# Expert weights in three 2 MB transfers per expert in place of ten

## What is computed

```python
xb = h[slot_tok].reshape(n_blocks, DISPATCH_BLOCK, D)
def expert_block(args):
    xe, e = args
    hid = jax.nn.silu(xe @ w_gate[e]) * (xe @ w_up[e])
    return hid @ w_down[e]
```

## Time and profile before

| | us |
|---|---|
| median of three runs (1152.67 to 1154.23) | 1153.86 |
| the profiled execution's own time | 1153.56 |
| its span | 1151.8 |
| TensorE matmuls busy in it | 1075.8 (93%) |
| 16 DMA engines, SyncE's queue | 62.6% of the span |

### The profile page before, as it was taken

The page is one execution under the profiler, slowest core; times in us unless marked ns, Lnnn a source line. Parts: engine busy times, 40 slices in busy tenths (PEclk is TensorE's granted clock), DMA queues, the critical chain, the costliest instruction groups (busy, mean ns, idle before and its releaser), DMA issues. The chain is left out here.

```text
span 1151.8 us, 17851 instructions
## 1 busy us (share of the span) xinstructions
PE 1075.8 (93%) x5269; PEld 616.3 (54%) x5270; DVE 513.6 (45%) x665; ACT 510.6 (44%) x690; POOL 290.6 (25%) x308
## 2 busy tenths in 40 slices
PE   5999996998999878999999999999999999969996
PEld 4899985877887532333333333333333333328885
DVE  5488999885232352123113213212311313356886
ACT  5444546663321264335345435535533625424332
POOL 2168776784000101011101011101111101023320
PEclk9999997999999788999999999999999999989999
DMA  8211941302132939999999999999999999965541
GB/s 264 66 55 39 287 129 74 116 19 92 74 135 90 345 141 394 396 376 338 398 395 357 396 397 362 398 398 386 369 396 396 364 395 399 403 222 188 194 147 41
DMA packets 149297, 300.32 MB, mean 261 GB/s; under 512 B 12032, under 2 KB 42784, under 8 KB 149259
## 3 DMA queue, kind: packets, MB, share of 16 engines
q1 hardware_dynamic: 134907, 264.69, 62.6%
q0 software_dynamic: 6512, 22.29, 5.6%
q10 hardware_dynamic: 7840, 12.85, 3.0%
HBM read 261.72 MB, written 38.06 MB: 260 GB/s over the span
## 5 line engine op out<-in xcount | busy, mean ns | idle before, releaser
L2012 PE MATMUL ps_gate_up<-weights,x_turned 128*64 128x512 f32 x1568 | 349.6, 598 | 1.7 <-issue 1.0
L106 ACT COPY weights<-raw_weights 128x2048 f32 (+1 forms) x99 | 186.0, 1899 | 102.7 <-issue 46.9
L2012 PEld LDWEIGHTS ps_gate_up<-weights,x_turned 128*64 128x64 f32 x1568 | 109.6, 137 | 207.2 <-issue 206.1
L106 DVE COPY weights<-raw_weights 128x2048 f32 x93 | 114.4, 1231 | 216.9 <-PE ps_gate_up L2012 83.0
L2025 PE MATMUL ps_y<-weights,h_turned 128*64 128x512 f32 x784 | 179.0, 598 | 0.9 <-ACT h_turned L1932 0.9
L439 POOL TENSOR_TENSOR conv_pool_taps<-conv_pool_taps,tap_product 128x448 f32<-128x448 f32 (+1 forms) x88 | 135.9, 1544 | 39.1 <-ACT tap_product L540 28.9
L115 POOL COPY token_ids<-item_tokens 128x1 int32 (+1 forms) x48 | 8.8, 183 | 446.2 <-PE ps_x L1999 446.2
L1972 DVE TENSOR_TENSOR hidden<-ps_gate_up,act_gate 128x256 f32<-128x256 f32 x49 | 20.8, 425 | 223.5 <-ACT act_gate L1923 210.6
L879 DVE SCALAR_TENSOR_TENSOR taps_bank<-a_ext,par,taps_bank 128x640 f32<-128x640 f32 (+1 forms) x128 | 101.5, 793 | 3.3
L2025 PEld LDWEIGHTS ps_y<-weights,h_turned 128*64 128x64 f32 x784 | 52.2, 136 | 93.3 <-issue 92.2
L540 ACT ACTIVATE tap_product<-a_ext,par 128x448 f32<-128x448 f32 (+1 forms) x104 | 75.4, 740 | 50.8 <-POOL conv_pool_taps L439 34.1
(11 more groups left out here) (285 smaller groups left out, 1560.2 us busy)
## 6 DMA issues: line engine op xcount, KB each, us to landing
raw_weights<-w_exp_gate SPq DMA_DIRECT2D x128, 512.0 KB, 12.0
raw_weights<-w_exp_up SPq DMA_DIRECT2D x128, 512.0 KB, 12.8
raw_weights<-w_exp_down SPq DMA_DIRECT2D x64, 1024.0 KB
y_rows<-y_tile ACTq DMA_DIRECT2D x98, 128.0 KB, 5.4
y_rows<-zero_rows SPq DMA_DIRECT2D x16, 512.0 KB, 6.2
x_rows<-x_tile SPq DMA_DIRECT2D x9, 512.0 KB, 2.6
h_rows<-h_tile SPq DMA_DIRECT2D x9, 512.0 KB, 2.9
mixer<-x_rows SPq DMA_DIRECT2D x9, 512.0 KB, 4.5
```

Of the source, the lines that this page charges most:

```text
L106: copy(S.work[s][:, :], raw).then_inc(S.w_ready[s], 1)
L2012: last = pe.matmul(ps_gu[side[j], :, :], x_t[:, c, side[of]], w[:, :, share(D_EXP, j)], start=(k == 0), stop=(k == KD - 1))
```

## The change

Gate and up of an expert come in two transfers of 2 MB (gate first, then up) which share one semaphore, and down comes in one of 2 MB with its own. All four copies of gate and up wait for both transfers of their group, both copies of down for theirs. SyncE issues the group of gate and up only when all four pieces of expert n-2 were copied and the whole group of n-1 has landed, and down in the same way. In `routing`, all of gate and up of expert 1 is issued at the late place, and down alone at the early one. The bytes, the rows of 2 KB (gate, up) and 4 KB (down) in `raw_weights`, and the copies stay.

```diff
+FIRST_OF = (0, 0, 0, 0, 4, 4)
...
-def load_piece(eng, S, s, n, slot, e):
-
+def load_weights(eng, S, pieces, n, slot, e):
+
+    first = pieces[0]
     if type(n) is not int or n >= 1:
-        eng.wait_ge(S.raw_loaded[s], n * LANDED[s])
+        eng.wait_ge(S.raw_loaded[first], n * LANDED[first])
+    for s in pieces:
+        if type(n) is not int:
+            eng.sem_inc(S.waits_met, 1)
+        if type(n) is not int or n >= 2:
+            eng.wait_ge(S.w_ready[s], n - 1)
...
+    raw = S.raw[:, slot, pieces[0]:pieces[-1] + 1, :].rearrange("p s n -> p (s n)")
+    if pieces == GU:
         for m in range(2):
-            eng.dma_start(raw.rearrange("p (k m n) -> p k m n", k=2, m=2)[:, :, m, :],
-                          S.w_experts[m][0, e, rows, :].rearrange("o (k p) n -> p (o k) n", p=P)).then_inc(S.raw_loaded[s], 16)
+            eng.dma_start(raw.rearrange("p (k m n) -> p k m n", k=KD, m=2)[:, :, m, :],
+                          S.w_experts[m][0, e, :, :].rearrange("o (k p) n -> p (o k) n", p=P)).then_inc(S.raw_loaded[first], 16)
     else:
...
+        eng.dma_start(raw.rearrange("p (k n) -> p k n", k=KE),
+                      S.w_experts[2][0, e, :, :].rearrange("o (k p) n -> p (o k) n", p=P)).then_inc(S.raw_loaded[first], 16)
...
-    eng.wait_ge(S.raw_loaded[s], n * LANDED[s] + LANDED[s])
+    eng.wait_ge(S.raw_loaded[FIRST_OF[s]], n * LANDED[s] + LANDED[s])
...
-                for s in (3, 4, 5):
-                    load_piece(sp, S, s, 1, 1, slice(1, 2))
+                load_weights(sp, S, DOWN, 1, 1, slice(1, 2))
...
-                for s in (0, 1, 2):
-                    load_piece(sp, S, s, 1, 1, slice(1, 2))
+                load_weights(sp, S, GU, 1, 1, slice(1, 2))
...
-                        for s in PIECES:
-                            load_piece(sp, S, s, n + odd, odd, bass.ds(e, 1))
+                        for pieces in (GU, DOWN):
+                            load_weights(sp, S, pieces, n + odd, odd, bass.ds(e, 1))
```

More of the change, by code:

```diff
@@ L72 @@
 PIECES = GU + DOWN
+FIRST_OF = (0, 0, 0, 0, 4, 4)
 LANDED = (32, 32, 32, 32, 16, 16)
-def load_piece(eng, S, s, n, slot, e):
+def load_weights(eng, S, pieces, n, slot, e):
+    first = pieces[0]
     if type(n) is not int or n >= 1:
-        eng.wait_ge(S.raw_loaded[s], n * LANDED[s])
+        eng.wait_ge(S.raw_loaded[first], n * LANDED[first])
[4 more added lines that the diff above has]
+            eng.wait_ge(S.w_ready[s], n - 1)
     if type(n) is not int:
         eng.sem_inc(S.waits_met, 1)
[L82 to L88, removed]
+    raw = S.raw[:, slot, pieces[0]:pieces[-1] + 1, :].rearrange("p s n -> p (s n)")
+    if pieces == GU:
         for m in range(2):
-            eng.dma_start(raw.rearrange("p (k m n) -> p k m n", k=2, m=2)[:, :, m, :],
-                          S.w_experts[m][0, e, rows, :].rearrange("o (k p) n -> p (o k) n", p=P)).then_inc(S.raw_loaded[s], 16)
-    else:
[L93 to L96, removed]
+            eng.dma_start(raw.rearrange("p (k m n) -> p k m n", k=KD, m=2)[:, :, m, :],
+                          S.w_experts[m][0, e, :, :].rearrange("o (k p) n -> p (o k) n", p=P)).then_inc(S.raw_loaded[first], 16)
+    else:
+        eng.dma_start(raw.rearrange("p (k n) -> p k n", k=KE),
+                      S.w_experts[2][0, e, :, :].rearrange("o (k p) n -> p (o k) n", p=P)).then_inc(S.raw_loaded[first], 16)
 def copy_piece(eng, S, n, s, items, on_act=None):
-    eng.wait_ge(S.raw_loaded[s], n * LANDED[s] + LANDED[s])
+    eng.wait_ge(S.raw_loaded[FIRST_OF[s]], n * LANDED[s] + LANDED[s])
     if items is not None:
@@ L379, in _ @@
                         sp.wait_ge(o_left, BLOCKS * PARTED)
-                        for s in PIECES:
-                            load_piece(sp, S, s, 0, 0, slice(0, 1))
+                        for pieces in (GU, DOWN):
+                            load_weights(sp, S, pieces, 0, 0, slice(0, 1))
                 for j in range(3):
@@ L1859, in _ @@
                         e = sp.value_load(S.expert_at[0:1, bass.ds(n + odd, 1)], min_val=0, max_val=EXPERTS - 1)
-                        for s in PIECES:
-                            load_piece(sp, S, s, n + odd, odd, bass.ds(e, 1))
+                        for pieces in (GU, DOWN):
+                            load_weights(sp, S, pieces, n + odd, odd, bass.ds(e, 1))
                 for s in range(4):
                     sp.wait_ge(w_ready[s], EXPERTS - 1)
-                    sp.wait_ge(S.raw_loaded[s], LANDED[s] * EXPERTS)
+                    sp.wait_ge(S.raw_loaded[0], LANDED[0] * EXPERTS)
                     sp.dma_start(S.raw[:, 0, s, :].rearrange("p (k n) -> p k n", n=D), ple_gate[:, 2 * s:2 * s + 2, :])\
@@ L1936, in gate_hi @@
                 def gate_hi(s):
-                    act.wait_ge(S.raw_loaded[s], LANDED[s] * EXPERTS + 16)
+                    act.wait_ge(S.raw_loaded[s], 16)
                     act.wait_ge(w_ready[s], EXPERTS)
@@ L1984, in _ @@
                 for n, s in enumerate((0, 1)):
-                    dve.wait_ge(S.raw_loaded[s], LANDED[s] * EXPERTS + 16)
+                    dve.wait_ge(S.raw_loaded[s], LANDED[0] * EXPERTS + 16 if s == 0 else 16)
                     dve.wait_ge(w_ready[s], EXPERTS)
```

## The result

The kernel with three transfers took 1199.63 us (median of 4 runs, 1197.57 to 1201.97) against 1153.26 us for the kernel before (4 runs, 1150.84 to 1154.23): 46.4 us more. The ratio on record is 1.0413 with a 95% interval of 1.0397 to 1.0429 (the two medians alone give 1.040). The forecast was 1188 us, with a range of 1168 to 1204. The profiled execution has a span of 1197.2 us, 45.4 above the 1151.8 of before. Lines 2012, 2032, 1972, 1923 and 1905 of before are 2010, 2030, 1970, 1921 and 1903 now.

What follows compares the result with a forecast made beforehand. The prediction took TensorE's own work as the bound, transfers only just quick enough. Terms 28.4 + 2.3 + 5 - 0.7 = 35 us on 1153.9 gave 1189, lowered by 1 for waits already there to 1188 us; range 1168 to 1204.

Steps and rivals of the forecast that it cites:

- Six tight places: Items 9, 17, 25, 33, 41 and 47: TensorE would idle 4 to 6 us ahead of the transposes there.
- The six places, 28.4 us: Next item starts 4.3 us late at four of the waits for weights, 5.6 at two: 28.4 us together.
- The fourth piece: At each of six waits, no copy starts before all four gate and up pieces land: 2.6 us each.
- the later issue of down: At each of six waits, down's issue also waits for VectorE's copy: 1.1 us, or 0 if the queue isn't dry.
- the second copy: At each of six waits, ScalarE's copy 0 now also comes behind the last landing: 1.9 us each.
- slack: Delay a landing can take before TensorE waits: 1.3 us at four of the six waits, 0 at two.
- The start, 2.3: Expert 1's gate and up land later with a fourth piece, delaying items 1 and 2: 2.3 us, 5 if later still.
- The clock, 0.8 a place, 5 us: TensorE's clock may fall behind each of six idle waits: 0.8 us each, 5 us in all, bounds 0 and 13.8.
- a full loss of the clock, 1197 us: Case where full clock loss alone, bounded by 2.3 us at each of six waits, gives 1197 us.
- The end, -0.7: At the barrier behind the stage, SyncE's last transfers and ScalarE's last store pass the delay through; 0.7 us taken off.
- SyncE's issues, 0: On SyncE, 3 issues per expert in place of 10 free a queue that nobody waits for: 0 us.
- The rival of a dry queue: Transfer queue runs dry between groups, 3 to 7 us a round more: 1205 to 1225 us, chance 0.13.

Runs made afterwards that it cites:

- silu ahead, ten transfers: Kernel before, ten transfers and a signal per piece, with silu, next tokens' copy and product put ahead of the copies for the next expert: 1151.59 us.
- the copies held back: Kernel before, its ten transfers issued as before, but each copy waits until all pieces of its group (gate and up, or down) have landed: 1183.75 us.
- every wait and ten transfers: Kernel before, ten transfers; copies wait for their whole group's landing, issues for its copying, and expert 1's piece 3 is issued late: 1193.85 us.
- the run with copy 2 moved: The changed kernel with ScalarE's copy 2 placed behind silu, the next tokens and copy 4; copy 0 stays ahead of silu: 1189.64 us.
- the run that held back only the issue: Kernel before, ten transfers; no piece of a group is issued before all pieces of that group in the same slot were copied: 1153.53 us.
- down alone joined: Kernel before with only down in one 2 MB transfer with one signal; gate and up stay in eight transfers with four signals: 1153.94 us.

## Why the prediction was right, and where it was not

- *TensorE bounds, the transfers are only just quick enough.* Right. With the waits gone (silu ahead, ten transfers) the stage runs at 11.56 us an item and not faster.
- *Six tight places, and only items 0 and 1 else.* Right: the waits stand at items 9, 17, 25, 33, 41 and 47 and at item 0.
- *The six places, 28.4 us.* 32.4 came. The terms can be read one by one from the start of ScalarE's first copy behind the landing. Counted from the start of its item and summed over the six places, it is 43.2 us before (the third piece), 57.5 with the copies held back, 63.0 with every wait and ten transfers, and 67.5 in the change:

| term at the six places | forecast, us | measured, us |
| --- | --- | --- |
| the fourth piece | 15.6 | 14.2 |
| the later issue of down | 6.6 | 5.6 |
| the size of the transfers | none | 4.5 |
| the second copy | 11.4 | 10.9 |
| slack | -5.2 | -2.9 |
| sum | 28.4 | 32.3 (32.4 but for rounding) |

- *The fourth piece, the second copy, the later issue of down.* Right in size. From the start of the copy to the transposes it takes 2.70 us with one copy ahead of silu (559.50 to 562.20 at item 9 of the run with copy 2 moved) and 4.49 with two (556.46 to 560.95): 1.8 for the second, where the prediction has 1.9. Down is issued 1.38 us into the item in place of 0.30.
- *Slack 1.3 at four places and 0 at two.* Right where it is 0, mis-sized at the four. The prediction has the next item start late from a landing 7.8 us into the item on. With one copy ahead of silu, the runs show it from about 7.45 on, and then late by what the landing lies behind that (7.80 gave 0.34, 7.79 gave 0.38, 7.99 gave 0.54). So the slack was 0.3 to 1.1 at the four places, 2.9 together; 1.3 had been read from one row, at one of the two best of them.
- *Missing: the size of the transfers.* The prediction gave it no term. It is 4.4 us in the starts of the items, the step from 28.4 to 32.8, and 4.5 in the landings.
- *Luck.* With ten transfers and every wait of the change the places came to 28.4 us, the figure of the forecast to the tenth. Landings and copies a little smaller than forecast and a slack that was smaller, too, cancelled out there.
- *The start, 2.3.* Mis-sized: 5.0. I put the landing at 441.8 from 10.6 us of transfer and 2.5 of delays; it took 16.1 us from the issue, not 13.1, and gate and up of item 1 then ran at half clock in part (9.49 us in place of 7.09), which the term left out. The upper end of 5 held it.
- *The clock, 0.8 a place, 5 us.* The term that was most off: 1.9 a place, 11.4 us, near my upper bound of 13.8. The prediction's figure for a full loss of the clock, 1197 us, is nearer to the result than its forecast. The row of 4.63 us of idle time was the nearest, and I discounted it because sparse work had gone before it. That reason did not hold.
- *The end, -0.7.* Mis-sized: the barrier's wait gave back 5.4 us. SyncE's tail of transfers, which made that wait, does not move with TensorE's delay in full: its last transfer is issued at 1002.1 before and at 1044.8 in the change, 42.7 us later, and lands 16.8 and 15.0 us behind its issue. In the change ScalarE's last store, issued at 1060.0, is then the last to land.
- *SyncE's issues, 0.* Right as far as seen: seven fewer issues for each expert gained nothing.

The misses of 4.0, 6.4 and 2.7 us on one side and 2.6 on the other make the 10.5 us between the sums (45.5 less 35); the mechanism and its places were right, and the median lies 11.6 us above the forecast, inside its range. The rival of a dry queue (1205 to 1225) lies above what was measured, and the run that held back only the issue shows no loss from it. The Trainium skill, "DMA: Bandwidth & Descriptors", section "Rules for kernel authors", asks for transfers of 1 MiB and more; here transfers of 0.5 MB fill the queue as well (396 GB/s), and the large ones cost 4.4 us.

## What to carry to other kernels

Joining transfers joins their signals: the first consumer then waits for the last byte, and whatever stands behind it on its in-order engine waits too. Before joining, find the places where the landing is on the path (here six of 49 items), and see what is queued behind the waiting copy; work that doesn't need the data belongs ahead of it. With that order, half the transfers cost nothing, and without it the same step costs 2%. And price an idle TensorE twice: once for the wait, once for the clock behind it.

## What the runs showed of the chip that I had not expected

What idle time stood ahead of a loss of clock. Over these kernels, at the six places, by the longest single pause of TensorE and by what gate and up took beyond 7.09 us behind it: idle under 1 us (16 cases) never lost anything. Idle of 1.76 to 2.58 us lost 1.4 to 2.8 us on the next item in 9 cases of 16, and 0.2 or less in 7, with no order by length (2.10 lost 2.76, 2.08 nothing). Of 31 cases of 2.68 us and more, 30 lost 1.4 to 2.7, and longer idle time did not cost more: 2.68 lost 2.58, 4.66 lost 1.36. The Trainium skill, "TensorE: Matmul & The Clock Gate", section "HAM oscillation — how this bites in real kernels", has waits for transfers throw the clock back each time; the traces agree for the six waits of the change, and not for 8 of the 47 pauses of 1.76 us and more.

A wait also has a tail: behind five of the six in the change TensorE stood still for another 0.7 to 1.0 us between the transposes and the next matmuls (0.72 at 562.36), and did so at full clock too (0.69 at 565.10). The sixth had none, in the change as in every run with such a wait there; its next item is written out behind the loop, where those of the other five are the loop's. At the others it sets in before TensorE waits for anything, and grows as the slack goes: 0.15 us with ScalarE's copy of the third piece 7.68 us into the item, 0.47 with 7.99 (down alone joined, items 41 and 9). What makes the pause is not shown; it is part of what "late" counts above.
